# Expert choice over 65 pair sums, TensorE four U steps ahead of the transposes, and another order of the first value transfers

## The reference, cut to what matters

```python
def peer(h, w_pq, sub_keys, u_tab, v_tab):
    q = (h @ w_pq).reshape(B, T, 8, 2, 64)
    s = jnp.einsum('bthcd,hckd->bthck', q, sub_keys)        # 128 scores per head and half
    top_s, top_i = lax.top_k(s, 16)
    cand = top_s[..., 0, :, None] + top_s[..., 1, None, :]  # 16 x 16 sums
    best_s, best_j = lax.top_k(cand.reshape(B, T, 8, 256), 16)
    i1 = take_along_axis(top_i[..., 0, :], best_j // 16)
    i2 = take_along_axis(top_i[..., 1, :], best_j % 16)
    expert = i1 * 128 + i2                                  # of 16384 experts
    w = softmax(best_s)
    # act = gelu(h . u_tab[expert]);  out = sum (act * w) * v_tab[expert]
```

## Time and profile before

| | us |
|---|---|
| median of 3 runs | 3266.9 (3266.49 to 3274.32) |
| profiled execution, own time | 3266.7 |
| its span in the trace | 3264.9 |
| PE busy in the span | 3020.8 (93%) |
| DVE busy | 2491.9 (76%) |
| ACT busy | 1539.1 (47%) |
| U steps of layer 0 (first to last block) | about 393 to 1074 |
| value phase of layer 0 | 1079 to 1605 |
| U steps of layer 1 | about 1864 to 2283 |
| value phase of layer 1 | 2283 to 2610 |

### The profile page before, as it was taken

The page is one execution under the profiler, slowest core; times in us unless marked ns, Lnnn a source line. Parts: engine busy times, 40 slices in busy tenths (PEclk is TensorE's granted clock), DMA queues, the critical chain, the costliest instruction groups (busy, mean ns, idle before and its releaser), DMA issues.

```text
span 3264.9 us, 49103 instructions
## 1 busy us (share of the span) xinstructions
PE 3020.8 (93%) x19164; PEld 2664.9 (82%) x19164; DVE 2491.9 (76%) x4940; ACT 1539.1 (47%) x2895; POOL 962.7 (29%) x883
## 2 busy tenths in 40 slices
PE   6998999989989999999879999898999999988898
PEld 4656799989989788888765899888998989755898
DVE  2696599897888688888758698997899865668653
ACT  3455435737557333333434547496555543232543
POOL 0000045555656344344000024455665300000000
PEclk9999999999999999999998999999999989977899
DMA  7384348968779999999437568899999967501444
GB/s 233 99 273 158 134 151 282 343 221 312 270 274 337 362 373 354 378 358 369 167 100 249 190 229 311 281 355 373 374 400 400 343 207 250 162 33 45 156 141 131
DMA packets 355495, 830.70 MB, mean 254 GB/s; under 512 B 21024, under 2 KB 217664, under 8 KB 335168
## 3 DMA queue, kind: packets, MB, share of 16 engines
q1 hardware_dynamic: 257216, 469.79, 41.4%
q0 software_dynamic: 95680, 353.46, 29.6%
q10 hardware_dynamic: 2368, 4.31, 0.4%
HBM read 750.90 MB, written 76.55 MB: 253 GB/s over the span
## 4 chain that ended last, share of the span: by engine, by line
PE 63%; DVE 24%; DMA 7%; ACT 4%; issue 2%; POOL 1%; DVEq 0%; SPq 0%; ACTq 0%; POOLq 0%
PE ps L1001 16%; PE ps L924 14%; PE ps L619 13%; DVE fr L1796 6%; DMA ring<-in_peer_v 4%; DVE area L1796 4%; DVE area L1804 4%; PE ps L980 3%; PE ps L1089 2%; PE ps L697 2%; PE ps L1081 2%; PE ps L853 1%; ACT fr L1245 1%; PE ps L636 1%; DVE acc L1796 1%
## 5 line engine op out<-in xcount | busy, mean ns | idle before, releaser
L1796 DVE TENSOR_TENSOR fr<-ring,fr 128x1024 fp32r<-128x1024 f32 x641 | 781.1, 1221 | 458.1 <-ACT fr L1245 443.1
L1245 ACT CAST fr<-ring 128x1024 fp32r<-128x1024 f32 x677 | 705.2, 1047 | 580.6 <-PE ps L1001 324.4
L924 PE MATMUL ps<-fr 128*128 128x384 f32 (+1 forms) x4784 | 852.2, 331 | 16.4 <-DVE fr L1796 16.4
L924 PEld LDWEIGHTS ps<-fr 128*128 128x128 f32 x4784 | 789.5, 192 | 22.6 <-DVE fr L1796 20.2
L1001 PE MATMUL ps<-fr 128*128 128x512 f32 x2304 | 525.3, 390 | 4.8 <-DVE fr L1796 4.8
L1001 PEld LDWEIGHTS ps<-fr 128*128 128x128 f32 x2304 | 434.5, 189 | 95.5 <-ACT area L1555 5.1
L619 PE MATMUL ps<-fr 128*128 128x256 f32 (+1 forms) x2928 | 416.9, 305 | 26.2 <-DVE fr L1796 26.2
L619 PEld LDWEIGHTS ps<-fr 128*128 128x128 f32 x2928 | 390.6, 194 | 52.3 <-DVE fr L1796 32.4
L2641 POOL DMA_INDIRECT plain<-in_peer_v,area x192 | 278.9, 1452 | 243.8 <-DVE area L1804 166.7
L2673 POOL DMA_DIRECT2D g_scratch<-area x256 | 145.1, 567 | 598.5 <-ACT area L1555 549.2
L1026 PE MATMUL ps<-fr 128*128 128x384 f32 x1024 | 301.9, 365 | 19.2 <-DVE fr L1796 18.4
(11 more groups left out here) (228 smaller groups left out, 4038.0 us busy)
## 6 DMA issues: line engine op xcount, KB each, us to landing
ring<-in_peer_uT SPq DMA_DIRECT2D x128, 1024.0 KB
ring<-in_peer_v SPq DMA_DIRECT2D x128, 1024.0 KB
ring<-in_w_mod SPq DMA_DIRECT2D x48, 1024.0 KB
w_scratch<-acc POOLq DMA_DIRECT2D x36, 1024.0 KB
g_scratch<-area POOLq DMA_DIRECT2D x128, 192.0 KB
area<-g_scratch POOLq DMA_DIRECT2D x64, 384.0 KB
area<-w_scratch POOLq DMA_DIRECT2D x16, 1536.0 KB
ring<-in_w_ada SPq DMA_DIRECT2D x24, 1024.0 KB
```

Of the source, the lines that this page charges most:

```text
L924: ins = e.matmul(o[:, 0:width], pairs[m][0], pairs[m][1], start=(m == 0), stop=(l == 0 and m == last), skip_group_check=l == 1)
L1245: e.copy(hi, x).then_inc(act.after(("high", name)), 1)
L1796: return e.tensor_tensor(o, a, b, op).then_inc(dve.after(*labels), 1)
```

## The change

It has three parts.

1. The pair sums. In place of 16 x 16 sums for each head there are 65, in five groups of at most 16 (`PAIRS`), and `best16` runs over 65 elements. All eight heads are summed by five operations before the first `best16`. The place of a sum now tells i and j in another way, so the arithmetic from place to number changes: two `tensor_scalar`, two copies of 8 elements, one subtraction of 120, two `scalar_tensor_tensor` and one cast, where there were two `tensor_scalar`, one copy and two casts. The comparison for the first number is with a row of steps and `is_ge`, and its values are differences.
2. `AHEAD_STEPS`. PE does four more U steps before it waits for ("ww", l, t), in both layers, and four fewer after the first score product of the next block. ACT does three more before it waits for the transposes in layer 1, and three fewer in the next search.
3. POOL's order at the end of the U steps, and of the first rows of V: `load_g(0)` and `load_w(0)`, with the waits ahead of them, come right after the last table store; the row gathers and stores of the first five steps stand behind them. The first rows of V are issued one per V tile, among the loads of `load_g` and `load_w`.

```diff
+PAIRS = [((1 << r) - 1, min(1 << r, 17 - (1 << r)), 16 >> r) for r in range(5)]
+WIDTH = 65
+AHEAD_STEPS = {"pe": (4, 4), "act": (0, 3)}
...
 # tensor_program, peer
-                fill(fill_a)
+                fill(fill_a - (early_steps if h4 == 0 else 0))
             fill(2 * fill_b)
             fill(2 * fill_c)
             if 128 * (t + 1) <= b.first:
                 continue
+            early_steps = AHEAD_STEPS["pe"][l]
+            fill(early_steps)
             w.wait_ge(dve, ("ww", l, t))
...
 # scalar_program, peer
-            fill(4 * fill_a + 2 * fill_b)
+            fill(4 * fill_a + 2 * fill_b - early_steps)
...
+            early_steps = AHEAD_STEPS["act"][l]
+            fill(early_steps)
             w.wait_ge(pe, ("ti", l, t))
...
 # vector_program, choose
+        cv = b.cand.rearrange("p (h x) -> p h x", h=8)
+        for r, (i0, ni, nj) in enumerate(PAIRS):
+            tt(cv[:, :, 16 * r:16 * r + ni * nj].rearrange("p h (a b) -> p h a b", a=ni),
+               tsv[:, :, 0, i0:i0 + ni].unsqueeze(3).to_broadcast([128, 8, ni, nj]),
+               tsv[:, :, 1, 0:nj].unsqueeze(2).to_broadcast([128, 8, ni, nj]), AD)
         for h0 in (0, 4):
-            cv = b.cand.rearrange("p (h a b) -> p h a b", h=4, a=16)
-            tt(cv, tsv[:, h0:h0 + 4, 0, :].unsqueeze(3).to_broadcast([128, 4, 16, 16]),
-               tsv[:, h0:h0 + 4, 1, :].unsqueeze(2).to_broadcast([128, 4, 16, 16]), AD)
-            best16([(b.cand[:, 256 * j:256 * j + 256], b.SW[j], ...
+            best16([(cv[:, h0 + j, 0:WIDTH], b.SW[j][:, 0:WIDTH], ...
...
-        ts(b.R1.bitcast(U32), b.BJ.bitcast(U32), 4, None, ALU.logical_shift_right, None)
-        ts(b.R2.bitcast(U32), b.BJ.bitcast(U32), 15, None, ALU.bitwise_and, None)
+        ts(b.R1.bitcast(U32), place, 1920, 19, ALU.bitwise_or, ALU.logical_shift_left)
+        ts(row, place, 4, None, ALU.logical_shift_right, None)
         e.tensor_copy(b.mxs, bs[:, :, 0]).then_inc(dve.after(), 1)
-        e.tensor_copy(b.R1f, b.R1.bitcast(U32)).then_inc(dve.after(), 1)
-        e.tensor_copy(b.R2f, b.R2.bitcast(U32)).then_inc(dve.after(), 1)
+        e.tensor_copy(ti_steps[:, :, 0], tiv[:, :, 0, 0]).then_inc(dve.after(), 1)
+        tt(ti_steps[:, :, 1:16], tiv[:, :, 0, 1:16], tiv[:, :, 0, 0:15], SU)
+        stt(low4, place, 15, row, ALU.bitwise_and, ALU.logical_shift_left)
+        stt(place, low4, 15, row, ALU.bitwise_and, ALU.logical_shift_right)
+        e.tensor_copy(b.R2f, place).then_inc(dve.after(), 1)
...
 # gpsimd_program, peer
-        fill(5)
         w.wait_ge(pe, ("ow", l, D // 4 - 1))
         w.wait_ge(dve, ("oh", l, D // 4 - 1))
         load_g(0)
-        fill(5)
         for i in range(2):
             w.wait_ge(M.w_stored[i], ("w", l, nst - 2 + i))
         load_w(0)
+        fill(5)
+        load_g(1)
+        fill(5)
+        load_w(1)
         fill(3)
-        load_g(1)
-        load_w(1)
-        fill(5)
         load_g(2)
         load_g(3)
         for _ in filling:
             pass
         w.wait_ge(pe, ("pu", l, 127))
-        for k in range(len(b.v_rows)):
-            v_row(k)
+        v_row(0)
         for a in range(128):
+            if a + 1 < len(b.v_rows):
+                v_row(a + 1)
             if a % 8 == 7:
                 load_w(a // 8 + 2)
```

More of the change, by code:

```diff
@@ L411, in peer @@
         b.TIf = lay.take(256).rearrange("p (h r) -> p h r", r=16)
-        b.cand = lay.take(1024)
+        b.cand = lay.take(640)
         b.rstd = b.cand[:, 0:512]
@@ L2131, in choose @@
+        for r, (i0, ni, nj) in enumerate(PAIRS):
+            tt(cv[:, :, 16 * r:16 * r + ni * nj].rearrange("p h (a b) -> p h a b", a=ni),
+               tsv[:, :, 0, i0:i0 + ni].unsqueeze(3).to_broadcast([128, 8, ni, nj]),
+               tsv[:, :, 1, 0:nj].unsqueeze(2).to_broadcast([128, 8, ni, nj]), AD)
+        last()
+        for h0 in (0, 4):
+            best16([(cv[:, h0 + j, 0:WIDTH], b.SW[j][:, 0:WIDTH], bs[:, h0 + j, :], bj[:, h0 + j, :]) for j in range(4)],
                    lambda i: fill(spread(fill_b, 5)[i], False))
@@ L2132, in choose @@
             fill(spread(fill_b, 5)[4], False)
[L2133 to L2135 removed]
+            last()
+        place, row, low4 = b.BJ.bitcast(U32), b.R2.bitcast(U32), b.R2f.bitcast(U32)
+        ts(b.R1.bitcast(U32), place, 1920, 19, ALU.bitwise_or, ALU.logical_shift_left)
+        ts(row, place, 4, None, ALU.logical_shift_right, None)
         e.tensor_copy(b.mxs, bs[:, :, 0]).then_inc(dve.after(), 1)
@@ L2146, in choose @@
         tt(ww, bs, b.mxs.unsqueeze(2).to_broadcast([128, 8, 16]), SU, ("wsub", l, t))
-        for c, (Rf, I) in enumerate(((b.R1f, b.I1), (b.R2f, b.I2))):
+        i2_values = tiv[:, :, 1, :]
+        for Rf, marks, op, values, I in ((b.R1, "steps", ALU.is_ge, ti_steps, b.I1),
+                                         (b.R2f, "iota", ALU.is_equal, i2_values, b.I2)):
             part = spread(fill_c, 6)
@@ L2828, in constants @@
     put("iota", np.arange(128)[None, :])
+    put("steps", np.arange(1, 17)[None, :] / 128.0)
     put("eps", np.array([[1e-6, 1e-5]]))
```

16 lines of the change are left out of this document (6 added, 10 removed).

## The result

The changed kernel takes 3243.48 us (median of 4 runs, 3242.71 to 3245.21) beside 3269.95 us for the kernel before (4 runs): a ratio of 0.9919, with a 95% interval of 0.9902 to 0.9936. A second set of 6 runs gave 3242.94 us and 0.9923. That is 26 us less where the forecast was 44. The profiled execution took 3242.74 us, its span is 3240.9 us against 3264.9, and the 24.0 us between the spans are what has to be placed.

What follows compares the result with a forecast made beforehand. TensorE, busy for 93% of the span, bounds the kernel; its idle time lies at the transposes, where VectorE ends last. 31 + 1 + 4 + 9 - 3 + 2 = 44 us from 3266.7 gives 3223 us, range 3206 to 3248.

Steps and rivals of the forecast that it cites:

- Part 1, sizes of the operations: VectorE's search operations in each choice: over 65 elements FIND_INDEX8, MATCH_REPLACE8 and MAX8 take 225, 215 and 222 ns.
- The saving of 8.3 us a choice: VectorE's work per choice: 7.7 + 2.45 - 1.1 - 0.7 = 8.3 us less, from shorter searches and fewer long sums.
- Sum for layer 0, "all three vanish: 24.0 us": TensorE's idle times in layer 0's three searches, 5.92, 10.64 and 7.44 us, all go; with other terms 31 us.
- Part 2, "18 products more ahead": TensorE's products ahead of the transposes: 18 more cover 3.1 us in layer 0; four steps cover 2.0 in layer 1.
- 2.2 behind the transposes and 4.9 of clock: Layer 0 behind the transposes: half of TensorE's idle in the last two blocks, 2.2 us, and slow clock, 4.9 us, go.
- Sum for layer 1, "against 8.3 + 2.0": Layer 1's searches: 4 us at the first transposes; at the second 10.3 against 11.76 us idle, limited by transfers to 9.
- Slower: Rival, chance 0.05: in the searches low parts follow ACT and TensorE, so VectorE's saving becomes waits and transposes come later; 3291 us.
- the cap of 8.9 us by the transfers: Layer 1's second search: 19.0 MB at 371 GB/s at most take 51.1 us, which allows 8.9 us of gain.
- Part 3: GpSimd's load order at the ends of the U steps: 1 us gain in layer 0, 3 us loss in layer 1.
- V rows, +2: Start of layer 1's value phase: one V row per tile lets the fifth activation read go earlier; 2 us gain.
- The rival of the transfers: Rival, chance 0.19: where searches end, waits for gathers take time back in both layers; 20.5 us left, 3246 us.
- The signs named for a wrong forecast: TensorE idle over 3 us at block 2's transposes; VectorE's search idle from ACT; value phase moving over 6, elsewhere over 2.

Runs made afterwards that it cites:

- the even fill: Layer 1 keeps 25 and 24 U steps, as before; with 65 sums, steps ahead, V rows one by one and old load order: 3233.8, again 3238.33 us.
- the uneven fill: 65 sums, steps ahead, V rows one by one, old load order, with layer 1's U steps 21 and 28 instead of 25 and 24: 3229.93 us, twice.

## Why the prediction came out as it did

The time lies in the range and the sign was right, but the sum had 18 us too many, and the time is only 4.5 us inside the upper bound. Layer 0 gave 22.4 of the 32 us forecast for it, layer 1 lost 2.1 in this trace where 10 were forecast, and the value phase of layer 1 gave 3.0 where 2 were. By its own steps, trace against trace:

- **Part 1, sizes of the operations**: right, each within 7 ns. The saving of 8.3 us a choice was about right too, once the holds by GpSimd are taken out: VectorE's busy time in the three searches fell by 9.0, 5.6 and 4.2 us, with holds of some 2.1, 5.7 and 4.4 us in them now and 1.6, 3.1 and 0 before, so by 8.2 to 9.5 us without them. The sum had no term for how two engines' operations fall on each other.
- **Sum for layer 0, "all three vanish: 24.0 us"**: 17.0 of 24.0 did. Behind the first two transposes 1.6 and 5.0 us went, where 1.2 and 3.5 were worked out, and the clock rose to 1.00. Block 2 had only 0.8 us to spare by the prediction's own count, and the holds took 3.5. Without them, and with the old order of the loads, V start is 30.7 us earlier, against 31 forecast.
- **Part 2, "18 products more ahead"**: the size was right and its share was not said. Counted alone by the prediction's own terms, three times 3.1 us, 2.2 behind the transposes and 4.9 of clock are 16.4 us, and alone it gave 15.7. The sums alone gave 10.9 and both 25.4, so the two hardly overlap. By itself this part was worth more than the sums, to which the prediction gave 8.3 of 11.4 us a block.
- **Sum for layer 1, "against 8.3 + 2.0"**: this is the step that failed. 4 and 9 us were forecast. The second search got 1.65 us shorter, by the steps ahead alone. Layer 1 as a whole gave 1.5 us with the steps ahead alone, and with the sums in and the even fill it was between 0.4 us shorter and 2.1 longer than before. A shorter choice counts only if VectorE is late for all that stands in its order. In layer 1 the low parts between its searches follow ACT, which follows TensorE, so VectorE gained nothing there; in the first search its waits for ACT grew as well, from 4.1 to 13.3 us. That is the mechanism of the rival *Slower*; it held for the whole of layer 1's saving and for most of block 1's, and it cost nothing, because TensorE was no later than before. The argument against it ("it is busy for 86.26 of 94.14") measured how little VectorE idled before, not how soon it would idle if it got faster: the cap of 8.9 us by the transfers was never reached.
- **Part 3**: the sign was wrong in layer 0 and is not settled in layer 1. Forecast +1, -3; measured -3 to -5 in layer 0 (-1.4 in the kernel before), between +1 and -2.5 in layer 1. The price in layer 0 is the gathers queued behind GpSimd's wait of 5.68 us, with VectorE waiting 11.37 us for them and TensorE coming back at a clock of 0.80. GpSimd's wait in layer 1 was 8.51 us, in the 8 to 11 forecast.
- **V rows, +2**: too low. VectorE's long wait at the start of layer 1's value phase is 1.45 us where it was 8.1, and the phase got 3 to 5 us shorter, though most of it moves 399 GB/s at a full share as in the earlier trace rows. So the start lent more time than it had to give back. This and the price of the loads about cancel, which is why the third part looked like nothing.
- **The rival of the transfers** had the number nearest to the result (3246), by another cause: no wait for a gather took back a gain in the searches, and the uneven fill moved the same bytes of layer 1 in 4.9 us less. That the time lies near it is luck.
- **The signs named for a wrong forecast**: VectorE's new idle time is put down to ACT, one of the signs that the prediction names, and here it points at the step that failed. TensorE idles 4.97 us in block 2's search, 2.24 of them at the transposes. Pieces outside the peer layers moved by more than 2 us too, but by no more than between traces of one kernel.

## What to carry to other kernels

When an engine's instructions stand in a fixed order, a saving on it is worth only its lateness at the next instruction that depends on another engine: list those instructions behind the saving, and see when their inputs are made, before you take the saving off someone else's wait. Work put ahead of a wait can be worth more than its own length, where the engine comes back at a lower granted clock (here 15.7 us for three times 3.1). Keep short issues (gathers) off a queue behind a wait for a landing. And price the parts of a change in the stage where each acts: two of them (4 us gained, 4 us lost) cancelled in the time of the whole kernel, and only the stages told them from nothing.

## What was not expected of the hardware

GpSimd's subtraction of 128x1024 elements (2.42 us) and VectorE's copies and two-operand operations exclude each other: an operation of 8 elements took 2400 ns, one of 1.22 us took 3.32, and GpSimd's own took 3.35 when VectorE was first. The search instructions ran beside it untouched. With the subtraction at 8 elements all were of normal length. And one stretch, from layer 0's first V product to layer 1's first scores, took 777.9 and 783.8 us in two traces of the same kernel (777.8 to 785.1 over all traces), which is more than most of the terms that were argued over here.
